# Rows of w_down spread over the partitions in fours, and activation transposes that read every fourth column

## The chip, the cores and the metric

The kernel runs on one core of one Trainium2 chip. The metric is the device time of one execution in microseconds. The times given are the median of several executions, with the lowest and the highest. The profile is of one execution, taken by the hardware profiler.

## The reference, cut to what matters

The model is one decoder layer on 256 tokens of width 1024: a mixer (a state-space branch and an attention branch) and then a sparse feed-forward layer with 32 experts. All of it is float32. The change touches only the second product of the experts:

```
gu = xb @ w_gu[e] + b_gu[e]                 # xb: rows of tokens, 1024 wide; w_gu[e]: 1024 x 2048
gate = min(gu[:, :1024], 7)
up = clip(gu[:, 1024:], -7, 7)
act = (up + 1) * gate * sigmoid(1.702 * gate)
y = act @ w_down[e] + b_down[e]             # w_down[e]: 1024 x 1024
out[token] += weight * y
```

Each token goes to 4 of the 32 experts.

## The kernel before

The kernel is written with explicit semaphores; each engine has its own program. After the mixer (to about 320 us) and the router comes the expert stage, a loop over items. An item is one expert with at most 64 of its tokens (CAP). Experts with more tokens get further items behind the 32; in the profiled execution there are 32 items in all.

**The ring.** Weights arrive in `ring`, 12 slots (SLOTS) of 128 partitions x 2048 float32, 1 MB each. An expert is 12 pieces: 8 of w_gu (GU_PIECES, one contraction step of 128 rows each, so that a partition gets one row of 8 KB) and 4 of w_down (DN_PIECES, two contraction steps, two rows of 4 KB per partition). The ring thus holds just one item. SyncE (SP) issues all these transfers, in `expert_load`: for each piece it waits on `w_used`, which TensorE raises by one when it is done with a piece, and then fills the slot again with the same piece of the next item. `expert_piece` gives the source of a piece. For the very first item some pieces go to memory beside the ring (`beside`), among them w_down's piece 9, which is loaded as two halves.

**An item on TensorE** (function `item`). The gathered tokens of the item lie in `hg`, features on the partitions, 64 tokens. The 64 columns fill half of the array, so the two halves of the output's columns are computed side by side, in the upper and the lower 64 partitions. In order:

1. bias of gate and up (L744), then 8 gate/up pieces of 4 matmuls each (L751). Between them stand the transposes and products that combine the item before (L713, L724);
2. the gather of the next item's tokens (L671), 48 short bf16 matmuls;
3. bias of the down product (L771);
4. four transposes of the activations `act_` (L779), once VectorE has made them (L1345 to L1351, with ScalarE's sigmoid, L923, in their midst);
5. ScalarE copies the transposed activations from PSUM to `actT` (L925);
6. 4 down pieces of 8 matmuls each (L788), then ScalarE copies the result out (L927).

`act_` has 128 partitions and 512 columns: partition 64h + s holds token s and the features 512h to 512h + 511. Transpose j takes 128 columns of it and gives `actT[:, j, h, :]` for both halves h. The down product's contraction step k (0 to 7) then multiplies `actT[:, k % 4, k // 4, :]` with rows of w_down: before, step k is the rows 128k to 128k + 127, and partition p holds row 128k + p, which matches column 128(k % 4) + p of `act_`.

Of the kernel before, what the change touches and what calls it, by code (L numbers as in the profile page):

```python
# [25 lines left out]
P = 128  # L26
# [64 lines left out]
def build(nc, x, c, w_ada, b_ada, g_mix, w_in, a_re, a_im, log_dt, b_re, b_im, c_re, c_im, ssm_d,  # L91
# [24 lines left out]
    ident = cst[:, C_ID:C_ID + P]  # L116
# [5 lines left out]
    def cut(n):  # L122
        at[0] += n
        assert at[0] <= zone.shape[1]
        return zone[:, at[0] - n:at[0]]
# [46 lines left out]
    act_ = cut(D // 2)  # L172
# [26 lines left out]
    ps = ctx.enter_context(nc.psum_tensor("ps", [P, 8, 512], F32))  # L199
# [101 lines left out]
    with nc.Block() as block:  # L301

        @block.sync
        def _(sp):
# [18 lines left out]
            def expert_piece(e, j):  # L323
                if j < GU_PIECES:
                    return w_gu[0, bass.ds(e, 1)].rearrange("e (k p) n -> p (e k) n", p=P)[:, j:j + 1, :]
                k = 2 * (j - GU_PIECES)
                return w_down[0, bass.ds(e, 1)].rearrange("e (k p) n -> p (e k) n", p=P)[:, k:k + 2, :]

            def beside(j):

# [18 lines left out]
            for j in range(SLOTS - RING0):  # L349
                n = PRE + RING0 + j  # L350
# [35 lines left out]
        def _(pe):  # L386
# [38 lines left out]
            for j in range(5):  # L425
                last = nc.tensor.transpose(ps[:, 6, ST * j:ST * j + ST], sprow[:, j, :], cst[0:ST, C_ID:C_ID + ST])
# [4 lines left out]
            for k in range(KD):  # L431
                for i in range(TT):
                    last = nc.tensor.transpose(ps[:, k // 2, (k % 2) * T + P * i:(k % 2) * T + P * i + P],
                                               xn_tok[:, i, P * k:P * k + P], ident)
# [144 lines left out]
            for n in range(2):  # L579
                take(place["ao", n])  # L580
                w = slot(place["ao", n], 4)
                for kk in range(KW):
                    for m in range(4):
                        last = mm(ps[:, 2 * n + m // 2, (m % 2) * T:(m % 2) * T + T], w[:, kk, P * m:P * m + P], oT[:, kk, :],  # L584
                                  start=(kk == 0 and m % 2 == 0), stop=(kk == KW - 1), skip_group_check=True)
# [5 lines left out]
                for k in range(KD):  # L591
                    t = (GT1, GT2)[n] + k
                    last = mm(ps[:, 4 + 2 * n + k // 4, P * (k % 4):P * (k % 4) + P], mod[:, t:t + 1].to_broadcast([P, P]), ident,
                              start=True, stop=True, skip_group_check=True)
# [3 lines left out]
            for n, b in enumerate((4, 6, 0, 2)):  # L598
# [6 lines left out]
                for kk in range(KW):  # L605
                    for m in range(4):
                        last = mm(ps[:, b + m // 2, (m % 2) * T:(m % 2) * T + T], w[:, kk, P * m:P * m + P], gluT[:, kk, :],  # L607
                                  start=(kk == 0 and m % 2 == 0), stop=(kk == KW - 1), skip_group_check=True)
# [23 lines left out]
            for i in range(TT):  # L632
                for n in range(4):
# [8 lines left out]
                    for kk in range(2):  # L642
                        k = 2 * n + kk
                        for h in range(2):
                            last = mm(ps[:, 4 + 2 * i + h, :], mergedT[:, k, P * i:P * i + P], w[:, kk, 512 * h:512 * h + 512],  # L645
                                      start=(k == 0), stop=(k == KD - 1))
# [32 lines left out]
            def further_items():  # L679


                pe.wait_ge(S["pos_sb"], 1)
                for j, src in enumerate((rt[:, 1], rt[:, 2])):
                    for i in range(TT):
                        last = nc.tensor.transpose(ps[0:EXPERTS, 3, T * j + P * i:T * j + P * i + P], src[:, i, :], ident)
                last.then_inc(S["rT_up"], 1)

                pe.wait_ge(S["extra_set"], 1)
                mm(ps[0:EXPERTS, 6, 1:2], cst[0:EXPERTS, C_TRI32:C_TRI32 + EXPERTS], chunk[:, 3:4], start=True, stop=True,
                   skip_group_check=True)  # L690
                mm(ps[0:1, 6, 2:3], ones[0:EXPERTS, 0:1], chunk[:, 3:4], start=True, stop=True,
                   skip_group_check=True).then_inc(S["cum_up"], 1)
                pe.wait_ge(S["rT_sb"], 1)

                pe.wait_ge(S["hot_set"], 1)
                for i in range(TT):
                    for a in (0, CAP):
                        t = P * i + a
                        mm(ps[a:a + CAP, 4, 16 * i:16 * i + OVER], rowT[:, 0, t:t + CAP], hot[:, 0, EXPERTS:ITEMS], start=True, stop=False,
                           skip_group_check=True)  # L700
                        mm(ps[a:a + CAP, 4, 16 * i:16 * i + OVER], ones[:, 0:CAP], hot[:, 1, EXPERTS:ITEMS], start=False, stop=True,
                           skip_group_check=True)
                        mm(ps[a:a + CAP, 5, 16 * i:16 * i + OVER], rowT[:, 1, t:t + CAP], hot[:, 0, EXPERTS:ITEMS], start=True, stop=True,
                           skip_group_check=True)
                mm(ps[0:1, 6, 8:8 + ITEMS], cst[:, C_E:C_E + 1], hot[:, 0, 0:ITEMS], start=True, stop=True,
                   skip_group_check=True).then_inc(S["item_up"], 1)

            def combine_weights(i):

                pe.wait_ge(S["pickw_set"], i)  # L710
                for t in range(TT):
                    for h in range(2):
                        last = nc.tensor.transpose(ps[:, 5, T * h + P * t:T * h + P * t + P], pickw[:, t, h, :], ident)  # L713
                last.then_inc(S["pwT_up"], 1)
# [11 lines left out]
            def item_piece(i, j, first):  # L726

                k = 1 if j < GU_PIECES else 2
                if not first:
                    pe.wait_ge(arrived[slot_of[j]], i * 16 + 16 * round_of[j])  # L730
                    return slot(PRE + RING0 + j, k)
                if j in ring0:
                    take(PRE + ring0.index(j))
                    return slot(PRE + ring0.index(j), k)
                pe.wait_ge(S[f"aside{j}"], 32 if j == 9 else 16)
                return None if j == 9 else aside[j].rearrange("p (k n) -> p k n", k=k)

            def item(i, first=False):


                pe.wait_ge(S["hotb_set"], i + 1)
                for b in range(2):
                    for h in range(2):
                        mm(ps[CAP * h:CAP * h + CAP, b, :], hotb, bgu_rows[:, D * b + 512 * h:D * b + 512 * h + 512],  # L744
                           start=True, stop=False, skip_group_check=True)
                pe.wait_ge(S["hg_sb"], i + 1)
                for j in range(GU_PIECES):
                    w = item_piece(i, j, first)
                    for b in range(2):
                        for h in range(2):  # L750
                            last = mm(ps[CAP * h:CAP * h + CAP, b, :], hg[:, j, :],  # L751
                                      w[:, 0, D * b + 512 * h:D * b + 512 * h + 512],
                                      start=False, stop=(j == GU_PIECES - 1), skip_group_check=True)
                    last.then_inc(w_used, 1)

                    if j == 1 and not first:
                        combine_weights(i)
                    if j == 3 and first:
                        further_items()
                    if j in (3, 4) and not first:  # L760
                        combine(i, j - 3)

                pe.wait_ge(S["pick_set"], i + 2)
                gather()

                if first:
                    pe.wait_ge(S["rT_sb"], 1)
                else:
                    pe.wait_ge(S["y_sb"], i)
                for h in range(2):  # L770
                    last = mm(ps[CAP * h:CAP * h + CAP, 3, :], hotb, bdn_rows[:, 512 * h:512 * h + 512],  # L771
                              start=True, stop=False, skip_group_check=True)
                if first:
                    last.then_inc(S["comb_up"], 2 * TT)
                pe.wait_ge(S["act_set"], i + 1)
                if first:
                    pe.wait_ge(S["item_sb"], 4)
                for j in range(4):
                    last = nc.tensor.transpose(ps[:, 4, P * j:P * j + P], act_[:, P * j:P * j + P], ident)  # L779
                last.then_inc(S["actT_up"], 1)  # L780
                pe.wait_ge(S["actT_sb"], i + 1)
                for j in range(DN_PIECES):
                    w = item_piece(i, GU_PIECES + j, first)
                    for kk in range(2):
                        k = 2 * j + kk
                        wk = halves[kk] if w is None else w[:, kk, :]
                        for h in range(2):
                            last = mm(ps[CAP * h:CAP * h + CAP, 3, :], actT[:, k % 4, k // 4, :], wk[:, 512 * h:512 * h + 512],  # L788
                                      start=False, stop=(k == KD - 1), skip_group_check=True)
                    last.then_inc(w_used, 1)  # L790
# [615 lines left out]
```

## Time and profile before

| | |
|---|---|
| median of 3 runs | 1347.08 us |
| lowest, highest | 1345.97, 1349.88 us |
| span of the profiled execution | 1347.3 us |
| TensorE busy | 1257.0 us, 93% |
| VectorE busy | 440.2 us, 33% |
| ScalarE busy | 147.1 us, 11% |
| moved by DMA | 459.90 MB, mean 341 GB/s |

The profiled execution's own time is its span, 1347.3 us from the first instruction to the last; no other time of it is recorded, and the span lies within the runs. The span is what the rows are measured in. PE is TensorE's matmuls, PEld its weight loads (which can run beside matmuls), DVE is VectorE, ACT is ScalarE, SP is SyncE; SPq are instructions of SyncE's queue. PEclk is the granted clock of TensorE as a share of 2.4 GHz. L779 is line 779 of the kernel.

### The profile page before, as it was taken

What the parts mean: (1) busy time and instruction counts of PE and PEld (TensorE: products, weight loads), DVE (VectorE), ACT (ScalarE), POOL (GpSimd) and SP (SyncE); (2) the same over time, 40 slices, a digit from 0 to 9 for tenths busy, and PEclk for the clock granted to TensorE, in tenths of its full rate; (3) what the DMA queues carried; (4) which work ended last, traced back from release to release, by engine and by line L of the source; (5) the groups of instructions that cost most, each with busy time, mean ns of one, the idle gap of its engine ahead of it and who ended that gap; (6) DMA issues with size and microseconds to landing.
All of it is one profiled execution on the core that took longest, in us unless ns stands there. A gap on an engine that the chain in (4) does not pass through costs nothing.

```text
span 1347.3 us, 17847 instructions
## 1 busy us (share of the span) xinstructions
PE 1257.0 (93%) x6924; PEld 541.0 (40%) x6924; DVE 440.2 (33%) x898; ACT 147.1 (11%) x253; POOL 99.4 (7%) x121
## 2 busy tenths in 40 slices
PE   5998999986999999999999999999999999999996
PEld 1765767843333333333333333333333333333332
DVE  3667781224222222222222222222222222222225
ACT  3001113131000000000000000000000000000001
POOL 2404651021000000000000000000000000000000
PEclk8999999996999999999999999999999999999999
DMA  9999124464699999999999999999999999999980
GB/s 343 388 406 336 65 92 156 155 224 156 250 376 407 405 396 383 398 399 393 395 401 404 398 396 402 402 394 400 404 399 385 391 391 401 405 399 400 399 327 32
DMA packets 95551, 459.90 MB, mean 341 GB/s; under 512 B 13564, under 2 KB 13800, under 8 KB 59656
## 3 DMA queue, kind: packets, MB, share of 16 engines
q1 hardware_dynamic: 94008, 458.50, 85.7%
q10 hardware_dynamic: 1520, 1.08, 0.3%
q8 instruction: 15, 0.25, 0.1%
q14 instruction: 8, 0.07, 0.0%
HBM read 458.51 MB, written 1.05 MB: 341 GB/s over the span
## 4 chain that ended last, share of the span: by engine, by line
PE 79%; DVE 7%; ACT 4%; issue 1%; DVEq 0%
PE ps L751 34%; PE ps L788 17%; PE ps L724 9%; PE ps L744 4%; PE ps L457 4%; PE ps L607 2%; PE ps L645 2%; DVE zone L1351 2%; DVE zone L1348 2%; DVE zone L1345 2%; PE ps L779 2%; ACT zone L923 2%; ACT zone L925 1%; PE ps L713 1%; PE ps L584 1%
## 5 line engine op out<-in xcount | busy, mean ns | idle before, releaser
L751 PE MATMUL ps<-ring,zone 128*64 128x512 f32 x2016 | 459.8, 598 | 0.0
L1334 DVE TENSOR_TENSOR zone<-zone,ps 128x512 f32<-128x512 f32 x124 | 85.3, 688 | 583.2 <-PE ps L724 583.2
L751 PEld LDWEIGHTS ps<-ring,zone 128*64 128x64 f32 x2016 | 136.7, 137 | 287.7 <-issue 287.7
L788 PE MATMUL ps<-ring,zone 128*64 128x512 f32 x1000 | 221.6, 595 | 21.6 <-ACT zone L925 21.6
L788 PEld LDWEIGHTS ps<-ring,zone 128*64 128x64 f32 x1000 | 69.0, 137 | 153.7 <-issue 124.5
L724 PE MATMUL ps<-zone 128*128 128x512 f32 x256 | 127.1, 619 | 1.1 <-ACT zone L917 0.9
L457 PE MATMUL ps<-hT,ring 128*128 128x256 f32 x448 | 103.1, 390 | 2.7 <-ACT hT L839 2.7
L457 PEld LDWEIGHTS ps<-hT,ring 128*128 128x128 f32 x448 | 86.3, 195 | 20.1 <-issue 8.4
L724 PEld LDWEIGHTS ps<-zone 128*128 128x128 f32 x256 | 43.3, 189 | 83.3 <-issue 81.5
L923 ACT ACTIVATE zone<-zone 128x512 f32<-128x512 f32 x32 | 20.2, 632 | 467.2 <-DVE zone L1345 467.2
L1345 DVE TENSOR_SCALAR zone<-ps 128x512 f32<-128x512 f32 x32 | 22.1, 692 | 149.4 <-PE ps L751 149.4
L744 PE MATMUL ps<-zone 128*64 128x512 f32 x256 | 61.8, 604 | 0.0
L671 PEld LDWEIGHTS ps<-zone 128*128 128x128 bf16 x1584 | 49.1, 99 | 27.1 <-issue 26.0
L671 PE MATMUL ps<-zone 128*128 128x64 bf16 x1584 | 53.1, 195 | 1.1 <-DVE zone L1262 1.1
L927 ACT COPY zone<-ps 128x512 f32<-128x512 f32 x32 | 18.8, 587 | 230.0 <-PE ps L788 230.0
L917 ACT COPY zone<-ps 128x512 f32<-128x512 f32 x32 | 18.8, 587 | 159.3 <-PE ps L713 159.3
L410 PE MATMUL ps<-ring,condb 128*32 128x512 f32 x192 | 28.1, 708 | 8.3 <-DMA ring<-in_w_ada 8.3
L771 PE MATMUL ps<-zone 128*64 128x512 f32 x128 | 34.5, 618 | 0.0
L744 PEld LDWEIGHTS ps<-zone 128*64 128x64 f32 x256 | 18.6, 140 | 36.7 <-issue 36.6
L779 PE MATMUL ps<-cst,zone 128*128 128x128 f32 x128 | 21.0, 286 | 12.7 <-DVE zone L1351 12.7
L1323 DVE TENSOR_SCALAR zone<-cst,posI,wI 128x64 f32<-128x64 f32 x128 | 31.3, 309 | 0.3 <-issue 0.3
L779 PEld LDWEIGHTS ps<-cst,zone 128*128 128x128 f32 x128 | 13.4, 140 | 40.9 <-DVE zone L1351 40.9
(285 smaller groups left out, 828.9 us busy)
## 6 DMA issues: line engine op xcount, KB each, us to landing
ring<-in_w_gu SPq DMA_DIRECT2D x252, 1024.0 KB, 7.8
ring<-in_w_down SPq DMA_DIRECT2D x125, 1024.0 KB, 7.1
ring<-in_w_ada SPq DMA_DIRECT2D x24, 1024.0 KB, 16.5
ring<-in_w_in SPq DMA_DIRECT2D x16, 1024.0 KB, 14.7
ring<-in_w_glu SPq DMA_DIRECT2D x4, 1024.0 KB, 11.5
ring<-in_w_out SPq DMA_DIRECT2D x4, 1024.0 KB, 4.7
zone<-in_w_gu SPq DMA_DIRECT2D x3, 1024.0 KB, 6.9
ring<-in_w_attn_o SPq DMA_DIRECT2D x2, 1024.0 KB, 14.2
```

What stands on the lines that cost most here:

```text
L457: last = mm(ps[:, b + m // 2, (m % 2) * T:(m % 2) * T + T], w[:, kk, P * m:P * m + P], hT[:, k, :], start=(k == 0 and m % 2 == 0), stop=(k ...
L671: last = mm(ps[:, 2, CAP * f:CAP * f + CAP], xpart[:, c, i, P * f:P * f + P], pick[:, i, :], start=(i == 0 and c == 0), stop=(i == TT - 1 ...
L724: mm(ps[:, 6 + h, :], pickwT[:, h, P * t:P * t + P], ysb, start=True, stop=True).then_inc(S["comb_up"], 1)
L744: mm(ps[CAP * h:CAP * h + CAP, b, :], hotb, bgu_rows[:, D * b + 512 * h:D * b + 512 * h + 512], start=True, stop=False, skip_group_check=True)
L751: last = mm(ps[CAP * h:CAP * h + CAP, b, :], hg[:, j, :], w[:, 0, D * b + 512 * h:D * b + 512 * h + 512], start=False, stop=(j == GU_PIECE ...
L771: last = mm(ps[CAP * h:CAP * h + CAP, 3, :], hotb, bdn_rows[:, 512 * h:512 * h + 512], start=True, stop=False, skip_group_check=True)
L779: last = nc.tensor.transpose(ps[:, 4, P * j:P * j + P], act_[:, P * j:P * j + P], ident)
L788: last = mm(ps[CAP * h:CAP * h + CAP, 3, :], actT[:, k % 4, k // 4, :], wk[:, 512 * h:512 * h + 512], start=False, stop=(k == KD - 1), ski ...
L923: nc.scalar.activation(sig, gate, ACT.Sigmoid, scale=ALPHA).then_inc(S["sig_set"], 1)
L1323: last = V.tensor_scalar(pickw[:, t, h, CAP * h:CAP * h + CAP], slots, posI[:, t, bass.ds(col, 1)], wI[:, t, bass.ds(col, 1)], ALU.is_equa ...
L1334: V.tensor_tensor(acc[:, t, 512 * h:512 * h + 512], acc[:, t, 512 * h:512 * h + 512], ps[:, 6 + h, :], ALU.add).then_inc(S["comb_add"], 1)
L1345: V.tensor_scalar(gate, ps[:, 0, :], LIMIT, None, ALU.min).then_inc(S["gated"], 1)
```

## The change

A w_down piece reads other rows. The 1024 rows are split in two halves h of 512 rows; in a half, partition p gets the four neighbouring rows 512h + 4p to 512h + 4p + 3 (q = 0 to 3). Contraction step k = 4h + q takes row 512h + 4p + q on partition p. A piece is two steps with neighbouring q, so each partition reads two rows that lie together, 8 KB, and from one partition to the next the source moves on by 16 KB. Pieces 0 and 1 read the first half of the matrix, pieces 2 and 3 the second. To match, transpose j (which is q now) takes columns j, j + 4, j + 8, ... of `act_`, 128 of them, at a step of 4 float32 or 16 bytes. Everything else is as it was: the number and size of transfers, slots, semaphores, matmuls, and the outputs of the transposes.

```diff
@@ -324,7 +324,7 @@
                 if j < GU_PIECES:
                     return w_gu[0, bass.ds(e, 1)].rearrange("e (k p) n -> p (e k) n", p=P)[:, j:j + 1, :]
                 k = 2 * (j - GU_PIECES)
-                return w_down[0, bass.ds(e, 1)].rearrange("e (k p) n -> p (e k) n", p=P)[:, k:k + 2, :]
+                return w_down[0, bass.ds(e, 1)].rearrange("e (h p q) n -> p (e h) q n", h=2, p=P)[:, k // 4, k % 4:k % 4 + 2, :]
@@ -776,7 +776,7 @@
                 if first:
                     pe.wait_ge(S["item_sb"], 4)
                 for j in range(4):
-                    last = nc.tensor.transpose(ps[:, 4, P * j:P * j + P], act_[:, P * j:P * j + P], ident)
+                    last = nc.tensor.transpose(ps[:, 4, P * j:P * j + P], act_[:, :].rearrange("p (n q) -> p q n", q=4)[:, j, :], ident)
                 last.then_inc(S["actT_up"], 1)
```

## Rows read from the trace of the kernel before

**Rows 1.** The page: busy time of TensorE; DMA share in 40 slices.

```profile
PE 1257.0 (93%) x6924; PEld 541.0 (40%) x6924; DVE 440.2 (33%) x898; ACT 147.1 (11%) x253; POOL 99.4 (7%) x121
...
DMA  9999124464699999999999999999999999999980
```

**Rows 2.** Chain of waits in order of time, 340 to 420 us: start, length, work.

```profile
366.68 5.33 PE ps L751 x24
...
398.33 5.33 PE ps L751 x24
```

**Rows 3.** The same chain, its last two items.

```profile
1284.52 5.33 PE ps L751 x24
1294.06 7.09 PE ps L788 x32
...
1316.17 5.33 PE ps L751 x24
1325.71 7.09 PE ps L788 x32
```

**Rows 4.** Stretches of the last two items: busy times, then clock, DMA share, GB/s.

```profile
1284.00:1300.00 16.00, 14.93 (x110) 5.77 (x110) 6.36 (x15) 1.22 (x2) 0.00 (x0) 1.00 0.93 376
1316.00:1330.00 14.00, 12.92 (x101) 5.20 (x102) 8.71 (x16) 1.22 (x2) 0.00 (x0) 1.00 0.01 2
```

**Rows 5.** Waits of TensorE's matmuls, 360 to 1310 us: total, times, longest (all rows).

```profile
PE ps L788 <- ACT zone L925: 20.3, 30, 0.7
PE ps L779 <- DVE zone L1351: 11.9, 30, 0.4
```

**Rows 6.** SyncE's transfers into the ring, 360 to 1320 us: lengths in ns, landings in us.

```profile
L341 SPq DMA_DIRECT2D ring<-in_w_down x120: 372/378/384, 378.3 to 1301.3; - x120
...
DMA to landing us min/median/max: 4.7/7.7/10.9
```

**Rows 7.** Stretches within one item, columns as in rows 4.

```profile
806.00:810.00 4.00, 4.00 (x14) 1.27 (x16) 1.57 (x3) 0.00 (x0) 0.00 (x0) 1.00 1.02 424
822.00:824.00 2.00, 2.00 (x12) 0.66 (x10) 0.00 (x0) 0.00 (x0) 0.00 (x0) 1.00 0.74 168
828.00:832.00 4.00, 4.00 (x22) 1.38 (x18) 0.00 (x0) 0.00 (x0) 0.00 (x0) 1.00 1.00 391
```

**Rows 8.** Timeline around one item's transposes: start, length, instruction, idle before it.

```profile
817.24 0.69 DVE L1351 SCALAR_TENSOR_TENSOR zone<-zone 128x512 f32<-128x512 f32 x1
...
817.98 0.42 PEld L779 LDWEIGHTS ps<-cst,zone 128*128 128x128 f32 x4 [1.28 <-DVE zone L1351]
817.98 0.66 PE L779 MATMUL ps<-cst,zone 128*128 128x128 f32 x4 [0.40 <-DVE zone L1351]
...
818.67 0.59 ACT L925 COPY zone<-ps 128x512 f32<-128x512 f32 x1 [2.20 <-PE ps L779]
...
819.31 0.20 PEld L788 LDWEIGHTS ps<-ring,zone 128*64 128x64 f32 x4 [0.91 <-ACT zone L925]
```

**Rows 9.** The page, DMA queues: packets, MB, share.

```profile
q1 hardware_dynamic: 94008, 458.50, 85.7%
```

**Rows 10.** Stretches with w_ada, then w_attn_o and w_glu in flight, as rows 4.

```profile
65.00:70.00 5.00, 5.00 (x25) 4.40 (x24) 4.59 (x13) 0.00 (x0) 0.00 (x0) 1.00 0.99 409
115.00:120.00 5.00, 5.00 (x28) 3.93 (x25) 4.13 (x7) 1.54 (x2) 4.76 (x4) 1.00 1.05 387
```

**Rows 11.** Timeline of two other groups of transposes, loads and matmuls (L426, L685).

```profile
17.21 0.48 PE L426 MATMUL ps<-cst,zone 16*128 16x16 f32 x5
...
17.21 0.38 PEld L426 LDWEIGHTS ps<-cst,zone 16*128 16x128 f32 x5 [1.48 <-issue]
...
328.05 0.61 PE L685 MATMUL ps<-cst,zone 128*32 128x128 f32 x4
```

**Rows 12.** Groups of weight loads by line: busy us, mean ns of one, idle before.

```profile
L779 PEld LDWEIGHTS ps<-cst,zone 128*128 128x128 f32 x128 | 13.4, 140 | 40.9 <-DVE zone L1351 40.9
...
L584 PEld LDWEIGHTS ps<-zone,ring 128*128 128x128 f32 x64 | 12.0, 190 | 3.3 <-issue 1.8
...
L685 PEld LDWEIGHTS ps<-cst,zone 128*32 128x32 f32 x4 | 0.3, 96 | 0.8 <-issue 0.8
```

## Prediction, made before the result was known

> **What bounds the kernel now.** I read the page first. TensorE is busy 93% of the span and the DMA engines are at nine tenths or more in nearly every slice from the twelfth on, at about 400 GB/s: both look full, and this change touches both [rows 1]. So the first question is which of the two ends last in an item of the expert stage, and the page alone does not say.
>
> The chain of waits does. From the first items to the last it holds TensorE, VectorE and ScalarE only, never a transfer, and it repeats to the hundredth: the run of 24 gate/up matmuls starts at 366.68 and 398.33, and at 1284.52 and 1316.17, that is 31.65 us per item at either end of the stage [rows 2, 3]. The last of these items runs while the DMA engines are all but idle (share 0.01, against 0.93 in the item before it), and from its 24 matmuls to its down projection it takes the same 9.54 us (1325.71 less 1316.17, 1294.06 less 1284.52) [rows 3, 4]. So neither waiting for data nor competition for memory is in the 31.65 us. The waits of TensorE between 360 and 1310 us say it again: they name VectorE (11.9 us) and ScalarE (20.3 us), no DMA [rows 5].
>
> How far is the stream from mattering? A ring slot is refilled when its piece is used up and is read again one item later, at the earliest 31.65 - 1.77 = 29.9 us on (a down piece is 8 of 32 matmuls that take 7.09 us [rows 3]). Transfers in this stage land at most 10.9 us after their issue [rows 6], so the latest still has 19 us to spare. The 12 transfers of an item move 12.58 MB; in 31.65 us that is 398 GB/s. Where 8 KB packets flow the stretch reads 424 GB/s, where mainly w_down's 4 KB packets flow 391, and once an item the queue runs nearly dry (share 0.74, 168 GB/s) [rows 7]. An item's transfers thus need 8 x 1.049/0.424 + 4 x 1.049/0.391 = 19.8 + 10.7 = 30.5 us of the 31.65. The stream is hidden, with large slack in time but only 4% in rate.
>
> The four activation transposes, though, lie wholly on the chain. At 817.98 TensorE starts them the moment VectorE's product is there, and it has nothing else to do; ScalarE's copy waits for them, and the down projection waits for that copy [rows 8].
>
> **The change, part by part.**
>
> *The w_down transfers.* Piece j of an expert now covers 128 runs of 8 KB at a pitch of 16 KB, instead of 256 rows of 4 KB. Same bytes, same 12 slots, same order and semaphores, and no DMA more: SP still issues four, at 0.38 us each [rows 6]. If source and destination are merged into one run per partition, 127 transfers lose 128 packets each (one of the 128 pieces is issued as two halves and stays at 4 KB), and queue 1's 94008 packets become about 77750 [rows 9]. At w_gu's 424 GB/s four pieces take 9.9 us in place of 10.7: 0.8 us an item that falls into idle time of the DMA engines, 0 on the path. The work that hides it is TensorE's 31.65 us; if that cover were gone, the 0.8 us would count, 25 us over 31 items. The bounds on the rate come from strided rows: w_ada, 8 KB runs at a pitch of 24 KB, flows at 409 GB/s; w_attn_o and w_glu, 2 KB runs at pitches of 4 and 8 KB, at 387 [rows 10]. At 387 the four pieces take 10.8 us and the item 30.6, still below 31.65. The point from which it decides is 4 x 1.049/(31.65 - 19.8) = 354 GB/s for w_down.
>
> *The down matmuls* read the same bytes of each slot and of actT in the same shapes: 0. The order of the contraction is permuted alike on both sides.
>
> *The transposes.* Each of the 128 (4 x 32 items) takes every fourth float32, a step of 16 bytes, where it read 128 neighbours. Which side is that, loaded or streamed? Where the source has 16 partitions and 128 columns, the weight load is 16*128 and the matmul streams 16x16: the activation is the loaded operand, the identity streams [rows 11]. So the cost is in LDWEIGHTS alone.
>
> No strided load is in the trace, so I bound it. Today's load of 128 columns takes 140 ns, one of 32 columns 96 [rows 12]: 44 ns for 96 columns, 0.46 ns a column, 59 ns of the 140 that grow with the columns. The five tiny transposes agree: their loads follow each other every (0.38 - 0.14)/4 = 60 ns [rows 11]. Low end: the step costs nothing. High end: a fetch now brings four neighbours at once and then brings one, so the 59 ns become 236, +177 ns. Between them lies the nearest row, a plain float32 load of 128 columns, which takes 190 ns where the transposing one takes 140 [rows 12]: the same instruction going over its columns at half the rate, +50 ns.
>
> How much of that shows? The first of an item's four loads has nothing over it (TensorE waits for VectorE): all of it. The other three are pulled under the matmul before. There the spacing of matmuls is (0.66 - 0.273)/3 = 129 ns with 128-column loads and (0.61 - 0.273)/3 = 112 with 32-column ones, 0.273 being the length of one such matmul [rows 8, 11]: 44 ns more of load made 17 ns of spacing, 38%. So +50 ns is 50 + 3 x 0.38 x 50 = 107 ns an item. I take this middle value: between ends as far apart as 0 and 177, the row of a load at half rate is the nearest to a slower load. Over 32 items 3.4 us. Bounds of this case: only the first load shows, 32 x 50 ns = 1.6 us; everything shows, 32 x 200 ns = 6.4 us. Nothing stands behind the transposes that would absorb it: behind them on TensorE's queue are the down matmuls, and ScalarE's copy and then everything of the item shifts alike. VectorE's work for the next item runs on beside the transposes, does not wait for them and is done long before TensorE asks.
>
> *Sum:* transfers 0, matmuls 0, transposes +3.4. The span of 1347.3 us is 0.2 above the median of the runs, so nothing lies around it worth adding: 1347.1 + 3.4 = 1350.5 us.
>
> The Trainium skill (Advanced Engine Details and Errata, SBUF Cachelines) has a rule against this change: a line holds 16 bytes, at least two hits on a line are needed to hide the memory's latency, and an access that finds a new line each time pays. Four float32 neighbours are one line and every fourth float32 is a new line each time. The page gives no price and no row here reads that way; by its rule the free case below is out and the sum is that of half or of quarter rate, while the rows seen so far, all of them contiguous, leave all three open.
>
> **The rivals.**
>
> *Free (35%).* The step costs nothing, because the load's address generator takes any step. For it: 140 - 59 = 81 ns of a load do not grow with its columns, and something can hide there. Against it: no strided load was seen. Time 1347.1, within 1 us.
>
> *Half rate (35%).* The sum above, 1350.5, from 1348.7 to 1353.5.
>
> *Quarter rate (22%), the rival on the slower side.* One mechanism: each column needs a fetch of its own where one served four, and the load (236 ns) outlasts the matmul before it, whose streaming takes at most 111 ns: a pair of 512-column matmuls takes 7.09/16 = 443 ns [rows 3], a quarter of it for 128 columns. The other 129 - 111 = 18 ns of a spacing stay. The first load shows 177, the others are spaced 236 + 18 = 254 ns instead of 129: 177 + 3 x 125 = 0.55 us an item, 17.7 us, 1365. If nothing overlaps, 4 x 177 = 0.71 us, 22.7 us, 1370. It decides from the point at which the load's growing part exceeds about 111 ns; up to there only the first load and the 38% count. For it: the granted clock is 1.00, 2.4 GHz, in the stage [rows 7], so 0.46 ns a column is about one a cycle, and reading neighbours may just be keeping up. Against it: nothing in the rows.
>
> *The stream becomes the bound (4%), also slower.* Runs at a 16 KB pitch touch only one half of the addresses at a time; if that halved w_down's rate to 212 GB/s, an item's transfers would need 19.8 + 19.8 = 39.6 us, 8 us more than TensorE, about 240 us over 30 items, near 1585. Against it: the strided rows at 387 and 409 GB/s, above the 354 at which it starts. [...]
>
> *Faster (4%).* Fewer packets could only help where TensorE waits for a transfer. In the expert stage it never does [rows 5], and what comes before that stage is untouched. I leave it for something the rows do not show.
>
> *The transfer does not change.* The two runs may stay two packets of 4 KB. The time would be that of the transposes' case all the same; this alters no chance.
>
> **How the numbers follow.** A measurement of this kernel tells about 0.3%, 4.0 us, from no change: 1343.1 to 1351.1. Free lies within. Of half rate's 35 I put 21 below 1351.1 and 14 above (the middle, 1350.5, is close to the edge, but the lower bound, where the overlap is complete, is well inside). Same 35 + 21 = 56; slower 14 + 22 + 4 = 40; faster 4. The range runs from 1346 (free, less the spread of the runs, 1346.0 to 1349.9) to 1367 (quarter rate with a little more showing), leaving out the stream case, the faster one and the far end of quarter rate, about 12 in 100.
>
> **What the profile after would show.** Queue 1 at some 77750 packets confirms the merged runs, 94008 denies them. The transposes' LDWEIGHTS at 140 ns: free; near 190: half rate; near 310: quarter rate. The four transposes at 0.66 us, at 0.7 to 0.85, or above 1.1. The item's period 31.65 plus exactly what the transposes gained; w_down landings no later than 11 us; no wait on a DMA. The forecast is wrong if the load is strongly slower than half rate, or if a wait of TensorE on the ring appears.

## The result and the profile after

| | before | after |
|---|---|---|
| median of 20 runs | 1348.41 us | 1351.01 us |
| lowest, highest | 1345.97, 1350.92 us | 1348.93, 1353.76 us |
| span of the profiled execution | 1347.3 us | 1351.8 us |
| packets of queue 1 | 94008 | 77752 |

The changed kernel takes 1.0021 times as long, with a 95% interval of 1.0013 to 1.0028: 1.8 to 3.8 us more, 2.8 in the middle. That is inside the 0.3% that were called no change, but the interval excludes 1: it is a small loss, not nothing. The forecast was 1350.5 us, 3.4 us more than the 1347.1 us that the kernel before had shown in three runs; over 20 runs its median is 1348.41.

The chain of waits of the changed kernel, in order of time (start, length, work), answers to [rows 2, 3]; the first line is from its stretch 340 to 420 us:

```profile
368.56 5.33 PE ps L751 x24
...
1298.46 7.09 PE ps L788 x32
...
1320.57 5.32 PE ps L751 x24
1330.19 7.09 PE ps L788 x32
```

From 368.56 to 1320.57 are 30 items, 31.734 us each. Before it was (1316.17 - 366.68)/30 = 31.650 [rows 2, 3]. An item has grown by 84 ns; 32 items make 2.7 us, the whole result. The spans differ by more, 4.5 us, but 1.9 of these lie before the 24 matmuls at 368.56, in the stages ahead of the item loop, where TensorE's mean granted clock over the first 100 us was 0.91 in this execution and 0.95 in the profiled one of before. The same mark stands at 365.83 to 367.22 in all the kernels below but moving_step and the three light ones. It is the spread between executions, and a reason to read an effect of 0.2% from the item and not from the span.

The timeline around one item's transposes, answering to [rows 8], shows where the 84 ns are:

```profile
821.04 0.56 PEld L779 LDWEIGHTS ps<-cst,zone 128*128 128x128 f32 x4 [1.27 <-DVE zone L1351]
821.04 0.74 PE L779 MATMUL ps<-cst,zone 128*128 128x128 f32 x4 [0.39 <-DVE zone L1351]
...
821.82 0.59 ACT L925 COPY zone<-ps 128x512 f32<-128x512 f32 x1 [2.29 <-PE ps L779]
...
822.46 0.20 PEld L788 LDWEIGHTS ps<-ring,zone 128*64 128x64 f32 x4 [0.87 <-ACT zone L925]
```

The loads take 0.56 us where they took 0.42, the matmuls 0.74 where they took 0.66, and ScalarE's copy waits 2.29 us for them, not 2.20. What follows is as it was. By line, the weight loads of the transposes (columns as in rows 12), with the transposes of L713 as a control that still reads neighbours:

```profile
L779 PEld LDWEIGHTS ps<-cst,zone 128*128 128x128 f32 x128 | 17.8, 208 | 40.7 <-DVE zone L1351 40.7
L713 PEld LDWEIGHTS ps<-cst,zone 128*128 128x128 f32 x128 | 13.4, 140 | 26.0 <-issue 26.0
```

At L779 208 ns against 140 before; at L713 still 140. The stream is where it was: the waits of TensorE's matmuls between 360 and 1310 us name no transfer, and the latest landing is 10.8 us, as answers to [rows 5, 6]. First the waits, then SyncE's transfers into the ring, then the page's queue line [rows 9]:

```profile
PE ps L788 <- ACT zone L925: 20.3, 30, 0.7
PE ps L779 <- DVE zone L1351: 11.8, 30, 0.4
```

```profile
L341 SPq DMA_DIRECT2D ring<-in_w_down x120: 332/333/333, 380.3 to 1305.7; - x120
...
DMA to landing us min/median/max: 5.0/7.9/10.8
```

```profile
q1 hardware_dynamic: 77752, 458.50, 85.3%
```

The packets have merged: 16256 fewer, which is 127 times 128. Even SyncE issues a w_down transfer faster, in 333 ns, the time that w_gu's need, instead of 378. Neither reaches the end of the kernel.

### The profile page after: what moved, and what is told of

It reads as the page before. It is cut to its first block, busy times and chain, and to the rows that moved or that the text cites. A ratio compares the mean times of both kernels' runs of the same rounds, so it can differ in the third digit from the quotient of the medians.

```text
span 1351.8 us, 17847 instructions
## 1 busy us (share of the span) xinstructions
PE 1261.1 (93%) x6924; PEld 546.3 (40%) x6924; DVE 442.1 (33%) x898; ACT 146.8 (11%) x253; POOL 99.6 (7%) x121
## 3 DMA queue, kind: packets, MB, share of 16 engines
q1 hardware_dynamic: 77752, 458.50, 85.3%
## 4 chain that ended last, share of the span: by engine, by line
PE 79%; DVE 7%; ACT 4%; issue 1%; DVEq 0%
PE ps L751 34%; PE ps L788 17%; PE ps L724 9%; PE ps L744 4%; PE ps L457 4%; PE ps L607 2%; PE ps L645 2%; PE ps L779 2%; DVE zone L1351 2%; DVE zone L1348 2%; DVE zone L1345 2%; ACT zone L923 2%; ACT zone L925 1%; PE ps L713 1%; PE ps L584 1%
## 5 line engine op out<-in xcount | busy, mean ns | idle before, releaser
L751 PE MATMUL ps<-ring,zone 128*64 128x512 f32 x2016 | 460.0, 598 | 0.0
L751 PEld LDWEIGHTS ps<-ring,zone 128*64 128x64 f32 x2016 | 136.7, 137 | 288.1 <-issue 288.1
L744 PE MATMUL ps<-zone 128*64 128x512 f32 x256 | 62.0, 606 | 0.0
L779 PE MATMUL ps<-cst,zone 128*128 128x128 f32 x128 | 23.9, 309 | 12.6 <-DVE zone L1351 12.6
L779 PEld LDWEIGHTS ps<-cst,zone 128*128 128x128 f32 x128 | 17.8, 208 | 40.7 <-DVE zone L1351 40.7
L744 PEld LDWEIGHTS ps<-zone 128*64 128x64 f32 x256 | 18.6, 140 | 36.7 <-issue 36.6
```

The lines of the kernel that those rows point to most:

```text
L751: last = mm(ps[CAP * h:CAP * h + CAP, b, :], hg[:, j, :], w[:, 0, D * b + 512 * h:D * b + 512 * h + 512], start=False, stop=(j == GU_PIECE ...
```

## The experiments

The theory after the result: all of the loss is the transposes' weight loads, most of it the first load of an item; the transfers neither help nor harm while TensorE sets the pace. The rival: part of it comes from the transfers at a 16 KB pitch. Beside it stood the question what exactly the load is charged for, and what the longer runs are worth once they are not hidden.

**One part of the change alone.** dma_only has the line of the diff in `expert_piece`, step_only the line in `item`. Each leaves out the other half, so the products pair activations with the wrong rows; the instructions and their amounts are the same.

> w_down is loaded in fours as in the changed kernel, the transposes read neighbours as before (so the down product pairs activations with the wrong rows of w_down; same instructions, same amounts). Theory (the transposes' loads are the whole loss, the transfers are hidden): queue 1 at 77752 packets, item period 31.65 us, ratio 1.000 within 0.001. Rival (the transfers at a 16 KB pitch disturb TensorE or arrive later): item period above 31.65, ratio above 1.001.

> The transposes read every fourth column, w_down is loaded as before (activations again paired with the wrong rows). Theory: the whole loss is here: loads of L779 at 208 ns, item period 31.74 us, ratio 1.002. Rival (the loss needs the transfers): 31.65 us and 1.000.

| | ratio to before | 95% interval | item |
|---|---|---|---|
| dma_only | 0.9997 | 0.9989 to 1.0006 | 31.646 us |
| step_only | 1.0015 | 1.0006 to 1.0024 | 31.734 us |
| both (the change) | 1.0021 | 1.0013 to 1.0028 | 31.734 us |

The items come from the first and the last gate/up run of the chain, dma_only first, then step_only:

```profile
366.03 5.33 PE ps L751 x24
...
1315.41 5.33 PE ps L751 x24
```

```profile
366.29 5.33 PE ps L751 x24
...
1318.31 5.33 PE ps L751 x24
```

The rival falls: with the new transfers and the old transposes the item is as before, with the old transfers and the new transposes it is as after.

**Which of the four loads shows.** The transposes of j = 0 alone, or of j = 1 to 3 alone, read every fourth column (condensed; in these two kernels the transposes stand in line 783):

```diff
+                    # first_only; last_three has j > 0
+                    src = act_[:, :].rearrange("p (n q) -> p q n", q=4)[:, j, :] if j == 0 else act_[:, P * j:P * j + P]
```

> Only the first of the four transposes of an item reads every fourth column, the others and w_down as before (activations paired with wrong rows). Theory (the first load of an item has no matmul over it and shows whole, 68 ns; the others are hidden): item period 31.65 + 0.07 = 31.72 us. Rival (the loss is spread over the four): +0.02 us, 31.67.

> The first transpose reads neighbours, the other three every fourth column (activations paired with wrong rows). Theory: the three are hidden but for what is left of 0.09 - 0.07: item period 31.65 to 31.67 us. Prediction's rule (38% of each shows): 3 x 0.38 x 0.068 = 0.08 us, 31.73. Rival (even spread): 31.72.

The chains, first_only and then last_three:

```profile
365.83 5.33 PE ps L751 x24
...
1316.84 5.33 PE ps L751 x24
```

```profile
366.54 5.33 PE ps L751 x24
...
1316.87 5.33 PE ps L751 x24
```

31.700 us and 31.678 us: the first load shows 50 ns, the other three together 28 ns, about 9 each. Both parts make 78, nearly the 84. Each kernel was profiled once; the period is a mean over 30 items. The expectations held in direction and not quite in size: the first load was to show 68 ns, and the other three at most 20 together.

The records of the four matmuls say which of them has its load uncovered (minimum, median and maximum in ns). First the kernel before with its other group of transposes, then first_only, then last_three:

```profile
L779 PE MATMUL ps<-cst,zone x128: 272/273/329, 343.2 to 1324.8; 128*128 128x128 f32 x128
L685 PE MATMUL ps<-cst,zone x4: 273/273/283, 328.0 to 328.4; 128*32 128x128 f32 x4
```

```profile
L783 PEld LDWEIGHTS ps<-cst,zone x128: 139/152/196, 342.3 to 1325.4; 128*128 128x128 f32 x128
L783 PE MATMUL ps<-cst,zone x128: 272/273/386, 342.3 to 1325.5; 128*128 128x128 f32 x128
```

```profile
L783 PEld LDWEIGHTS ps<-cst,zone x128: 137/205/212, 343.1 to 1325.4; 128*128 128x128 f32 x128
L783 PE MATMUL ps<-cst,zone x128: 282/284/329, 343.1 to 1325.5; 128*128 128x128 f32 x128
```

With only the first load slower, only the maximum moves, 329 to 386 ns; with only the other three slower, the maximum stays and the median moves. The mean of before, 286 ns, is that of three records of 273 and one near 329 in every four. So the longest record is the first matmul's, and it includes the wait for its load. That load grew by 56 ns (140 to 196) and its matmul by 57; the other three loads grew by 65 to 69 ns. With 329 ns for the first matmul the four of before are spaced (0.66 - 0.329)/3 = 110 ns, not 129. The group with 32-column loads is spaced (0.61 - 0.283)/3 = 109 ns, the same. The prediction read a share of 38% for the later loads out of the difference between these two groups; that difference, 0.05 us in all, is the first load's 44 ns, seen once. Measured, the three later loads show 28 ns of about 3 x 68, which is 14%.

**What the load is charged for.** pairs spreads the rows in twos, which gives the same runs of 8 KB and a step of 8 bytes; step3 and step16 change only the step (step16 also the table that is read). The lines are cut to the expressions.

```diff
+ w_down[0, bass.ds(e, 1)].rearrange("e (g p q) n -> p (e g) q n", g=4, p=P)[:, k // 2, :, :]
+ act_[:, 256 * (j // 2):256 * (j // 2) + 256].rearrange("p (n q) -> p q n", q=2)[:, j % 2, :]     # pairs
+ act_[:, 0:384].rearrange("p (n q) -> p q n", q=3)[:, min(j, 2), :]                               # step3
+ bgu_rows[:, :].rearrange("p (n q) -> p q n", q=16)[:, j, :]                                      # step16
```

> Computes the reference. Rows of w_down spread in twos: partition p gets rows 256g + 2p and 256g + 2p + 1, again one run of 8 KB, and the transposes read every second column, a step of 8 bytes. Theory (a load pays when each column lies in another stretch of 16 bytes, and two columns in one are enough): loads at 140 ns, item period 31.65 us, ratio 1.000, packets 77752. Rival (each step above one costs in proportion to the stretches touched, 64 in place of 32 against 128 at step four): loads near 140 + 68/3 = 163 ns, item period 31.68.

> All four transposes read every third column (wrong columns; 12 bytes, not a power of two; w_down as before). Theory A (any step but one): 209 ns, item period 31.73 us. Theory B (it matters whether two columns can share an aligned stretch of 8 bytes, or the step is even): a value between 140 and 209 ns.

> The transposes read 128 columns at a step of 16 float32, 64 bytes, from the table of expert biases (2048 columns) in place of the activations; they still start when the activations are ready. The down product is of other numbers, the same in amount. Known so far: 209 ns for a load at a step of 4 and at a step of 2. Theory A (the price is for any step but one, once): 209 ns, item period 31.73 us. Theory B (wider steps cost more): above 230 ns, and more than 31.78.

The loads of L779 (minimum, median and maximum in ns), in pairs, step3 and step16:

```profile
L779 PEld LDWEIGHTS ps<-cst,zone x128: 194/209/223, 343.7 to 1327.8; 128*128 128x128 f32 x128
```

```profile
L779 PEld LDWEIGHTS ps<-cst,zone x128: 188/199/218, 342.6 to 1326.1; 128*128 128x128 f32 x128
```

```profile
L779 PEld LDWEIGHTS ps<-cst,zone x128: 186/196/208, 342.6 to 1325.8; 128*128 128x128 f32 x128
```

A step of 8 bytes costs what one of 16 costs, 209 ns; 12 bytes 199, 64 bytes 196. Between the first and the last run of 24 gate/up matmuls the items follow: pairs (1319.24 - 367.22)/30 = 31.734 us, step3 (1317.58 - 366.09)/30 = 31.716, step16 (1317.24 - 366.10)/30 = 31.705. Pairs came out at 1.0018 (1.0009 to 1.0027) of the kernel before, and both its theory (140 ns) and its rival (163 ns) were wrong. For step3 and step16 the theory "any step, once" named 209 ns and 31.73 us, a little too much, and the rival of step16 (above 230 ns) falls. Among the four steps measured the price comes with leaving the neighbour; it does not grow with the step, nor with the number of 16-byte stretches that are touched. That the steps of 2 and 4 are 10 ns and more dearer than the other two is seen but not explained. Whether the 55 to 70 ns are paid once a load or column by column is not shown: every strided load here has 128 columns.

The rule that two hits on a 16-byte line are enough (Advanced Engine Details and Errata, SBUF Cachelines, in the Trainium skill) foretells that a step of four pays, and the trace agrees (208 ns against 140). It also foretells that a step of two is free, and here the measurement decides against it (209 ns).

**Moving the step elsewhere.** Can the rows be spread without a step in the loads? permuted_write lets VectorE's last operation store its columns sorted (it reads neighbours and stores 512 bytes apart), moving_step lets TensorE stream the columns of w_gu and of the bias in that order. Both compute the reference. (First the line of permuted_write, then that of moving_step, whose L751 is line 752.)

```diff
+                V.scalar_tensor_tensor(act_.rearrange("p (q n) -> p n q", q=4), up.rearrange("p (n q) -> p n q", q=4), 1.0,
+                                       gate.rearrange("p (n q) -> p n q", q=4), ALU.add, ALU.mult)
+                last = mm(ps[...].rearrange("p (q n) -> p q n", q=4), hg[:, j, :],
+                          w[:, 0, D * b + 512 * h:D * b + 512 * h + 512].rearrange("p (n q) -> p q n", q=4), ...)
```

> Computes the reference. w_down in fours; VectorE's last operation of the activation (L1351, on the chain, 693 ns) writes its columns sorted by their remainder modulo four, and the transposes read 128 neighbours. Theory (a write at a step costs VectorE nothing): L1351 at 693 ns, item period 31.65 us, ratio 1.000. Rival (each read or write at a step of 16 bytes or more halves its rate): L1351 near 1.25 us, 0.55 us an item, 18 us, ratio 1.013.

> Computes the reference. w_down in fours, and the activations come out of TensorE already sorted: the gate and up products and their biases stream their 512 columns in the order of the remainder modulo four (a step of 16 bytes on the streamed operand instead of the loaded one; 2048 + 256 matmuls), so that the transposes read neighbours. Theory (a float32 matmul streams 512 columns in about 430 ns, two cycles a column, and has time for any step): matmuls of L751 and the item as before, 31.65 us, ratio 1.000. Rival (any step but one costs a streamed column what it costs a loaded one, 69/128 = 0.54 ns): 0.28 us more for each pair of matmuls, 36 pairs an item, 10 us an item, a ratio near 1.23.

Permuted_write took 1.0089 of the kernel before (1.0076 to 1.0103), moving_step 1.3996 (1.3973 to 1.402). First L1351 in permuted_write, by line; then moving_step's matmuls of the gate/up products, by line, and its chain:

```profile
L1351 DVE SCALAR_TENSOR_TENSOR zone<-zone 128x512 f32<-128x512 f32 x32 | 33.2, 1038 | 1.1
```

```profile
L752 PE MATMUL ps<-ring,zone 128*64 128x512 f32 x2016 | 932.1, 1080 | 0.0
```

```profile
1800.00 10.96 PE ps L752 x24
...
1848.55 10.96 PE ps L752 x24
```

VectorE's operation grows by 345 ns, from 693, and all but a few ns of it show: the item is (1326.62 - 366.87)/30 = 31.99 us. The half-rate price that the rival named (550 ns) was too high, and free it is not. On the streamed side a step is dearest: 12 pairs of matmuls take 10.96 us instead of 5.33, 0.47 us more a pair or 0.92 ns a column. An item has 36 such pairs, 32 of L751 and 4 of L744 (in the trace each product of the code is two matmul instructions, so a gate/up piece has 8 of them and not 4): 16.9 us more, an item of 48.55 us. The expectation that a float32 stream has time for any step was plainly wrong, and its rival, priced from the load, was too low by more than a third. Whether another step would cost the stream as much was not tried.

**The transfers without their cover.** light_before, light_after and light_pairs leave out part of TensorE's work (two of three gather products and the up half of gate/up), so that the stream sets the pace. The code is cut to the two loops.

```diff
-                        for c in range(3):
+                        for c in range(1):          # gather
...
-                    for b in range(2):
+                    for b in range(1):          # gate/up products of an item
```

> The kernel before with TensorE's work in an item cut: the up half of the gate/up products is left out (only its bias is kept) and the gather uses one of its three bf16 parts; transfers as before. TensorE's own 31.65 us fall to about 31.65 - 3.5 - 1.0 = 27.1. Theory: the stream becomes the bound and an item takes the 30.5 us of its transfers (8 pieces at 424 GB/s, 4 at 391), landings grow to near 20 us and TensorE waits for the ring. Rival (the stream has more to give than the rates seen): nearer 29.7, all pieces at 424 GB/s.

> The changed kernel with the same cuts of TensorE's work. Prediction's theory: with the cover gone the runs of 8 KB are worth 0.8 us an item: 29.7 us against 30.5 of the same cuts on the kernel before, about 24 us in all. Rival (runs of 8 KB at a pitch of 16 KB flow no faster than two rows of 4 KB; the stretches of the changed kernel in which w_down flows read 307 to 398 GB/s): no gain, or a loss.

> The same cuts of TensorE's work as in the two kernels with a light TensorE (no up half, one of three bf16 parts of the gather), with rows of w_down spread in twos: runs of 8 KB as in fours, but each transfer of 1 MB without gaps. Known so far: 29.45 us an item with two rows of 4 KB, 29.18 with runs of 8 KB at a pitch of 16 KB, where 0.8 us had been expected between them. Theory A (the 4 KB packets never cost 0.8 us; 0.27 is what packets cost): 29.2 us, ratio to the kernel before as the fours, 0.939. Theory B (packets of 8 KB are worth 0.8 us and the pitch of 16 KB takes 0.5 back): 28.7 us, ratio near 0.928.

| | ratio to before | item, once the stream sets the pace | mean of all 31 steps |
|---|---|---|---|
| light_before | 0.9452 (0.9436 to 0.9468) | 30.12 us | 29.45 us |
| light_after | 0.9388 (0.9373 to 0.9404) | 29.83 us | 29.18 us |
| light_pairs | 0.94 (0.9384 to 0.9416) | 29.83 us | 29.18 us |

The items do not all take the same time, and the mean over all of them misleads. The starts of down products in the chains, light_before, light_after and light_pairs (three items lie between the first two lines of light_before, five between those of light_after):

```profile
337.20 8.78 PE ps L788 x32
...
414.92 8.78 PE ps L788 x32
...
617.56 3.68 PE ps L788 x16
...
1099.49 3.68 PE ps L788 x16
```

```profile
337.34 8.78 PE ps L788 x32
...
466.76 8.78 PE ps L788 x32
...
555.48 8.78 PE ps L788 x32
...
1241.47 8.78 PE ps L788 x32
```

```profile
526.84 8.65 PE ps L788 x32
...
1242.67 8.78 PE ps L788 x32
```

The first items take (414.92 - 337.20)/3 = 25.9 us in light_before and (466.76 - 337.34)/5 = 25.9 in light_after: there TensorE finds nearly all its pieces in the ring. Then an item takes (1099.49 - 617.56)/16 = 30.12 us in light_before, (1241.47 - 555.48)/23 = 29.83 in light_after and (1242.67 - 526.84)/24 = 29.83 in light_pairs. For the 12.58 MB of an item 30.12 and 29.83 us are 418 and 422 GB/s, just what the stretches below read. The 29.45 and 29.18 that the expectation of light_pairs names are means over both kinds of item.

In this later part TensorE waits for the ring, as this row of light_before's waits between 360 and 1310 us says, and the stretch 600 to 900 us (columns as in rows 4; light_before, then light_after) shows the stream full:

```profile
PE ps L751 <- DMA ring<-in_w_gu: 91.0, 103, 1.4
```

```profile
600.00:900.00 300.00, 246.41 (x1080) 76.97 (x1077) 80.34 (x170) 23.29 (x39) 0.00 (x0) 0.96 1.02 418
```

```profile
600.00:900.00 300.00, 248.84 (x1087) 79.09 (x1084) 81.22 (x170) 23.86 (x40) 0.00 (x0) 0.96 1.01 422
```

With the cover gone the longer runs do gain, 1274.64 to 1266.67 us, 8 us. That is 0.3 us an item over the 26 or so that the stream paces, under half of the 0.8 that was forecast for each. The expectation of light_before lay near: 30.12 us, between its 30.5 and the rival's 29.7. The pitch of 16 KB takes nothing back: pairs, whose transfers have no gaps, has the same 29.83. Theory B of light_pairs falls. The slower loads of the transposes should cost nothing where TensorE waits for data anyway. No light kernel with the new transfers and the old transposes was run, but light_after's stream is full.

## Why the prediction was right, point by point

- **What bounds the kernel.** Right. Items in step with TensorE, no wait on a transfer, and dma_only at 1.000.
- **The transfers, 0 on the path; 77752 packets.** Right. The cover was read well too: 30.5 us were worked out for an item's transfers, light_before's steady items take 30.12. The gain in it was mis-sized: 0.8 us an item were forecast, 0.3 measured. With light_after's 422 GB/s for w_gu's eight pieces, the four of w_down take 30.12 - 19.9 = 10.2 us, an estimate of 411 GB/s for 4 KB rows. The 391 was read soon after the queue's dip [rows 7] and is no capacity. So the gain without cover is 8 us and not 25.
- **The activation is the loaded operand.** Right; the loads grew by 68 ns, and only those of L779. The matmuls grew too, from 273 to 283 ns (median).
- **Half rate, +50 ns.** The first load of an item grew by 56 ns and showed 50, the others grew by 65 to 69. If all of it lies in the part that grows with the columns, that part went from 59 to 127 ns, a little over twice; no run separates this from a fixed charge a load.
- **38% of the others.** Mis-sized. 3 x 0.38 x 50 = 57 ns were expected, 28 measured. The reading behind the share was wrong: it took the first of the four matmuls to last 0.273 us like the others, and it lasts 0.329, because its load is uncovered. With that the two groups are spaced alike, 110 and 109 ns, and the 17 ns a spacing are gone. What was right is that a slower load under a matmul shows in small part; the 14% come from the runs and not from those rows.
- **The sum.** 107 ns an item against 84, 3.4 us against 2.7. The first load's 50 were right, the excess is the share of the others, less what was lost by pricing their load at +50 and not +68. That the measured median lies only 0.5 us from the forecast is partly luck: the sum started from 1347.1 us, and the kernel before has a median of 1348.41 over 20 runs. Forecast was +3.4 us, measured +2.8. The choice itself was open: half rate and free had 35% each.
- **Quarter rate, the stream as the bound, free.** None happened. The quarter rate would have shown as 310 ns a load; at 208 its growing part, 127 ns, is only little past the 111 at which, by the prediction, it begins to outlast the matmul before it. The 16 ns of that difference are more than the 9 that each of the later loads shows; the picture is argued and not shown.
- **Nothing lies around the span.** Wrong. The profiled execution of the changed kernel took 1353.69 us with a span of 1351.8; every run has about 1.8 us around it. The profiled execution of before was therefore not the median of its three runs. It shifts both kernels alike and changes no term of the sum.

What stays open: why steps of 2 and 4 cost at least 10 ns more than steps of 3 and 16, whether the price is by the load or by the column, and the 6 ns between the two parts measured alone (78) and together (84).

## What to carry to other kernels

Before a transfer is made more efficient, find out whether anything waits for it; here DMA engines that looked full (nine tenths and more in every slice) drew 398 GB/s where 418 were to be had, 5% more, and a gain of 8 us in the stream was worth nothing while the access pattern that paid for it was on the chain. A layout that leaves the neighbour has to be paid somewhere, and of the three places tried the cheapest is an operand that is loaded, seldom, and under something else: 84 ns an item in the transposes' loads, 345 ns in VectorE's store, 16.9 us in the streamed operand. An effect of 0.2% is read from the period of a loop over 30 rounds, where a difference of 30 ns shows, before it is read from medians. But look first whether the period is the same throughout: in the light kernels the mean over all items mixed 26 and 30 us.

## What was not expected of the hardware

- A float32 matmul that streams 512 columns at a step of 16 bytes took 1079 ns instead of 592 (medians), and a pair of them 0.91 us instead of 0.44.
- A transposing load of 128 float32 columns took 209 ns at a step of two as at a step of four, against 140 for neighbours.
- A transfer whose rows merge into one run of 8 KB is issued by SyncE in 333 ns, one of two rows of 4 KB in 378.
- With TensorE waiting up to 1.4 us several times an item, its mean granted clock in the stage was 0.96 and not 1.00. This stretch of light_after has most of one such fall, on a DMA stream that does not change (columns as in rows 4):

```profile
596.00:600.00 4.00, 1.78 (x10) 0.63 (x11) 0.00 (x0) 0.58 (x1) 0.00 (x0) 1.00 1.01 422
600.00:604.00 4.00, 4.00 (x8) 1.18 (x4) 0.58 (x1) 0.00 (x0) 0.00 (x0) 0.57 1.01 420
604.00:608.00 4.00, 4.00 (x13) 1.22 (x14) 2.10 (x4) 0.00 (x0) 0.00 (x0) 1.00 1.02 426
```

The mean of 0.57 is close to the lower level, 1.2 GHz; TensorE had been busy for 1.78 of the 4 us before. In four-microsecond steps it did 8 matmuls where it then did 13.
